# Gathering the second half of the next expert's rows behind the last up product, in a one-core mixture-of-experts kernel

## What is computed

```python
y = rmsnorm(h, norm_mix_g[0]);  h = h + mixer_gmlp(y, ...)
y = rmsnorm(h, norm_ffn_g[0])
probs = softmax(y @ router_w)              # 16 experts, 4 groups of 4
# each token: best group, two experts of it, weights gw
for e in range(16):
    xblk = rows of y routed to expert e
    hid = silu(xblk @ w_gate[e]) * (xblk @ w_up[e])    # 2048 -> 1024
    out[rows] += gw * (hid @ w_down[e])                # 1024 -> 2048
return rmsnorm(h + out, final_g)
```

## Time and profile before

| | us |
|---|---|
| median of 3 runs | 1259.27 |
| lowest, highest | 1258.11, 1261.31 |
| the profiled execution, own time | 1261.97 |
| its span, first to last instruction | 1259.9 |
| PE matmuls busy | 1172.1 (93%) |
| PE weight loads busy | 550.4 (44%) |
| DVE busy | 391.1 (31%) |
| ACT busy | 155.6 (12%) |
| DMA moved | 460.28 MB, mean 365 GB/s |
| mean granted PE clock | 0.980 |

### The profile page before, as it was taken

One profiled execution on the slowest core, in us unless ns is written; L12 is line 12 of the kernel. 1 busy time (PEld: TensorE's weight loads), 2 busy tenths in 40 slices (PEclk: granted clock), 3 DMA queues, 4 the chain that ended last, 5 costly groups with the idle time before them and its releaser, 6 DMA issues.

```text
span 1259.9 us, 13384 instructions
## 1 busy us (share of the span) xinstructions
PE 1172.1 (93%) x5217; PEld 550.4 (44%) x5217; DVE 391.1 (31%) x589; ACT 155.6 (12%) x231; POOL 6.4 (1%) x26
## 2 busy tenths in 40 slices
PE   7799999999999999999999998999998998999986
PEld 5688888887333333333332333333333333333322
DVE  4777788776402121120212020211202020211123
ACT  1212001011110110101011010101010101010002
POOL 0000001000000000000000000000000000000000
PEclk9899999999999999999999999999999999999998
DMA  9756555596899799999999999999999999999995
GB/s 337 263 189 200 194 174 156 178 367 265 342 375 424 323 425 423 424 424 424 424 423 425 423 425 422 426 422 425 422 425 422 426 423 424 424 424 424 423 425 227
DMA packets 73925, 460.28 MB, mean 365 GB/s; under 512 B 9368, under 2 KB 10928, under 8 KB 24496
## 3 DMA queue, kind: packets, MB, share of 16 engines
q1 hardware_dynamic: 71536, 458.28, 89.9%
q10 hardware_dynamic: 2368, 1.71, 0.4%
HBM read 457.86 MB, written 2.10 MB: 365 GB/s over the span
## 4 chain that ended last, share of the span: by engine, by line
PE 72%; DMA 21%; DVE 3%; ACT 2%; ACTq 1%; issue 1%; SPq 0%; DVEq 0%
PE bank L1078 26%; DMA ring<-in_moe_w_up 18%; PE bank L1119 13%; PE bank L902 7%; PE bank L903 7%; PE bank L904 7%; PE bank L1054 7%; PE bank L1033 3%; DMA more_slots<-in_moe_w_up 2%; ACTq L418 1%; PE bank L1107 1%; DVE sil L822 1%; DVE sil L820 1%; ACT sil L507 1%; ACT sil L510 1%
## 5 line engine op out<-in xcount | busy, mean ns | idle before, releaser
L1078 PE MATMUL bank<-ring,xg 128*64 128x512 f32 x1664 | 402.8, 595 | 24.5 <-DMA ring<-in_moe_w_up 24.5
L1078 PEld LDWEIGHTS bank<-ring,xg 128*64 128x64 f32 x1664 | 127.0, 137 | 259.6 <-issue 231.4
L902 PE MATMUL bank<-w_hi,act_hi 128*128 128x512 f32 x384 | 153.7, 400 | 8.0 <-DVE w_lo L573 7.2
L903 PE MATMUL bank<-w_lo,act_hi 128*128 128x512 f32 x384 | 151.5, 394 | 0.0
L904 PE MATMUL bank<-w_hi,act_lo 128*128 128x512 f32 x384 | 151.4, 394 | 0.0
L1119 PE MATMUL bank<-ring,sil 128*64 128x512 f32 x640 | 140.0, 592 | 0.0
L794 DVE TENSOR_TENSOR acc<-acc,bank 128x512 f32<-128x512 f32 x136 | 85.9, 683 | 138.1 <-PE bank L1054 137.4
L573 DVE TENSOR_TENSOR w_lo<-ring,w_hi 128x1024 fp32r<-128x1024 f32 x96 | 117.7, 1226 | 3.3
L1078 PE MATMUL bank<-more_slots,xg 128*64 128x512 f32 x384 | 112.7, 592 | 0.3 <-DMA more_slots<-in_moe_w_up 0.3
L804 DVE COPY x_row<-bank 128x512 f32<-128x512 f32 x16 | 11.1, 691 | 301.8 <-PE bank L1033 300.6
L1054 PE MATMUL bank<-y,back 64*128 64x512 f32 x272 | 93.9, 635 | 0.0
(11 more groups left out here) (162 smaller groups left out, 478.0 us busy)
## 6 DMA issues: line engine op xcount, KB each, us to landing
ring<-in_moe_w_gate SPq DMA_DIRECT2D x112, 1024.0 KB, 23.6
ring<-in_moe_w_up SPq DMA_DIRECT2D x96, 1024.0 KB, 23.6
ring<-in_moe_w_down SPq DMA_DIRECT2D x80, 1024.0 KB, 20.8
more_slots<-in_moe_w_up SPq DMA_DIRECT2D x32, 1024.0 KB, 25.9
more_slots<-in_moe_w_down SPq DMA_DIRECT2D x32, 1024.0 KB, 26.1
ring<-in_a_w_in SPq DMA_DIRECT2D x31, 1024.0 KB, 5.3
ring<-in_a_w_out SPq DMA_DIRECT2D x16, 1024.0 KB, 5.4
more_slots<-in_moe_w_gate SPq DMA_DIRECT2D x16, 1024.0 KB, 28.1
```

The lines of the kernel that those rows point to most:

```text
L902: T.matmul(dst, hi, wh, start=(k == 0), stop=False)
L903: T.matmul(dst, hi, wl, start=False, stop=False)
L1078: ins = T.matmul(bank[c][at:at + TOK, :], xg[:, 2 * m + s, :], slot(slot_of(2 * m + up))[:, s * F + c * BANK:s * F + (c + 1) * BANK], star ...
```

## The change

The second half of an item's rows is prepared one item earlier. On PE, `gather(1)` for the next item moves from behind m = 0 to behind m = 7, ahead of the wait for `hid`; `transpose_rows(i + 1, 1)` moves from behind m = 1 to behind the third down product (f = 2). In the last item both are left out. On DVE the copy of the second half, now `take_second_row(i + 1)`, comes behind the gated product, ahead of `take_half(i + 1, 0)`, with one added wait: the transposes of the first half must have read `x_row`. `take_half(i + 1, 1)` follows it. For item 0 both engines do this work ahead of their loops. The instructions in total are the same.

```diff
 # DVE
+            def take_second_row(n):
+                dve.wait_ge(gathered, n * 2 + 2)
+                dve.wait_ge(row_transposed, n * 2 + 1)
+                V.tensor_copy(x_row[:, :], bank[7][:, :]).then_inc(row_b_ready, 1)
+
             def item(i, last=False):
-                dve.wait_ge(gathered, i * 2 + 2)
-                V.tensor_copy(x_row[:, :], bank[7][:, :]).then_inc(row_b_ready, 1)
...
                 ins.then_inc(place_ready, 1)
-                take_half(i, 1)
...
                 else:
+                    take_second_row(i + 1)
                     take_half(i + 1, 0)
-
+                    take_half(i + 1, 1)
+
+            take_second_row(0)
+            take_half(0, 1)
             with dve.Fori(0, last_item) as i:
...
 # PE
                     ins.then_inc(step_done, 1)
-                    if m == 0:
-                        gather(1)
-                    if m == 1:
-                        transpose_rows(i, 1)
...
                             gather(0)
+                if not last:
+                    gather(1)
                 pe.wait_ge(hid_ready, i + 1)
...
                     ins.then_inc(step_done, 1)
-
+                    if f == 2 and not last:
+                        transpose_rows(i + 1, 1)
+
+            gather(1)
+            transpose_rows(0, 1)
             with pe.Fori(0, last_item) as i:
```

## The result

The changed kernel takes 1264.03 us (median of 7 runs, 1263.54 to 1265.03) against 1259.27 us before: 4.8 us slower, ratio 1.0037 with a 95% interval of 1.0026 to 1.0049. The forecast was 1264.8.

What follows compares the result with a forecast made beforehand. Weight stream taken as the bound behind 424 us, its restart set by PE's early work: 8.2 later start plus 2.4 slow clock, less 2 x 1.72 gathers and 1.70 dip, gives +5.5 on 1259.27, 1264.8 us; range 1260.5 to 1268.5.

Steps and rivals of the forecast that it cites:

- The bound: Whole loop: PE sets the pace up to about 424 us; behind that weights stream without pause at 424 GB/s.
- Rival 1: All items: PE is the bound and the freed wait is gain, 16.9 us faster, 1242.4 us; chance 0.05.
- The start: Ahead of the loop: PE waits for DVE's copy, idle 5.8 us, so item 0's m = 0 starts 8.2 us later.
- Rival 2: Ahead of the loop: the wait is absent or small; with none, 2.0 us faster, 1257.2 us; chance 0.06.
- its break-even: Start of item 0's m = 0: a shift of 5.1 us breaks even, so a start before 321.5 is a gain.
- The clock: Behind PE's idle time ahead of item 0: the clock falls to half rate and costs 2.4 us, ends 0 and 3.1.
- rival 3: Start of item 0: the clock holds and the 1.15 us partly goes; +1.9 to +3.1, 1261.2 to 1262.4 us; chance 0.20.
- The items: Item 0's m = 0 to item 1's step 12: two hidden gathers and one dip less, 100.39 us instead of 105.53.
- rival 4: Wait for `hid`: the gather doesn't hide and the dip stays; 10.6 us slower, 1269.9 us; chance 0.07.
- The waits and the stream: Queue dry at 425.4, next issue at 427.4, no pause behind; PE's waits for up units grow from 24.5 to some 55 us.
- The pauses one by one: The weight stream's four early pauses: first grows 10.6 us, second (1.0) goes, third shrinks 0.7, fourth 3.4; together +5.5.
- The median: Whole kernel: the sum of +5.5 us put on the median of 1259.27 gives 1264.8 us.

Runs made afterwards that it cites:

- the busy items: Changed kernel with 7 dummy products on PE behind m = 0 of every item: 1268.59 us, ratio to the kernel before 1.007.
- the halved transfers: Kernel before and changed kernel, each with half the bytes per weight transfer from item 3 on (wrong weights): 1227.23 us and 1198.18 us.
- the copy amid the tables: Changed kernel with DVE's copy of item 0's second half moved from behind the tables to the middle of them: 1258.8 us, ratio to before 0.999.
- filling the wait: Changed kernel with 22 dummy products in PE's wait ahead of item 0: 1264.3 us; with the last item's waits filled too: 1263.13 us.
- the new order: SP issues units 12 to 18 ahead of 7 to 11 for items 1 and 2: kernel before 1259.34 us; item 0 written out, gather ahead, 1252.53 us.

## Why the prediction was right

**The bound.** A DMA share of 1.01 behind 424 us, not PE's 93%, decides: shown by the busy items (28 us of work, 4.6 us of time) and by the halved transfers, where the same change is worth 29.1 us. Rival 1 is out.

**The start.** Forecast 8.2 us and 5.8 us of idle PE; measured 8.55 with 0.44 of it by the slow clock, and 5.58. Rival 2 (no wait) didn't happen, but its break-even held: the copy amid the tables starts m = 0 ahead of 321.5 and is a small gain.

**The clock.** Forecast 2.4 us, 2.15 in the profile, so rival 3 is out as to the products' times. The 2.4 was a choice between two rows, 1.70 and 3.1, and no sum, so that it came this close is in part luck. In time this term is the weakest: filling the wait brought back 0.3 us in one kernel and 1.2 us in the other, and the early copy showed some 1.6 of the 2.15.

**The items.** From m = 0 to step 12 of item 1, 100.39 was forecast; 426.90 - 324.95 - 1.71 = 100.24 was measured. The gather hides (rival 4 is out) with 0.40 us to spare, and the dips behind `hid` are gone.

**The waits and the stream.** The queue was to run dry at 425.4, and by 1 us windows it did at about 425.2 (share 0.85, 0.22 and 0.00 from 424 on); the issue was forecast for 427.4 and came at 426.90. PE's waits for up units were to be some 55 us and are 54.4. No new pause opened in the changed kernel. The pauses one by one came less exactly: +10.1, -1.0, +0.2 and -4.0 us against +10.6, -1.0, -0.7 and -3.4, which sum to +5.3 against +5.5.

**The median.** The sum gave +5.5; +4.76 was measured. 0.5 us of the difference is in the issue, which came that much earlier than forecast: 0.25 by the clock term, the rest by the start of m = 0 and the way from there to step 12. The other 0.2 us are within the interval of the medians. One thing the prediction left out: from m = 3 of the last item on, PE's only wait for weights is the 0.51 us at m = 7, so a dip there would have counted.

## What to carry to other kernels

Where weights stream at full rate and PE waits for them, find the last moment at which the stream stood still and the instruction that released it: here only PE's work ahead of that moment counted, whatever its busy share, and at the far end the stretch in which the last weights are used up. Moving work one iteration earlier gives the first iteration a prologue, and its place in the other engines' order (here one copy behind a chain of tables) can cost more than the loop saves ahead of that moment. If the order of a queue is changed, reckon every unit behind the edit with its own wait: in both kernels here the pauses that the new order closed came back in part or in full a few units on.

## What the runs showed of the hardware

Behind a wait of PE of 5.58 us the clock was at 1.2 GHz from 324 to 328 and 2.15 us were lost; behind one of 6.08 us 2.8 us were lost in m = 0; behind one of 0.85 us nothing was lost on the way to the issue (420.01 - 319.54 = 100.47 us against 100.24). In the kernel before with halved transfers, the same wait of 2.1 us was followed by a slow stretch in some items only (down products of 15.65 and 13.95 us in neighbouring items); with the wait at 0.40 us, as in the changed kernel, there was none in any of its 15 items. The Trainium skill, "TensorE: Matmul & The Clock Gate", section "HAM oscillation — how this bites in real kernels", describes a kernel whose PE falls back to the lower clock at each wait for a transfer. The rows here agree with it, though the waits are for DVE: 1.2 GHz behind the wait of 5.58 us. From SP's issue to data moving in an empty queue it took about 1 us: with the issue at 330.13 the share was 0.00 up to 331 and 0.77 in the microsecond behind it, with the one at 426.90 it was 0.00 up to 427, then 0.51, and 1.02 from 429 on.
